# Weights of a mixture of experts in three rings and one halved slot, an attention stage joined with the projections behind it, and a router worked out block by block

## The reference

```python
def second_block(x, ...):
    for l in range(2):
        z = x @ w_in                      # c_q, c_kv, k_rope, sb_qkv, conv_in, fox_qkv, fox_f, gates
        y_a = _mla(...)                   # softmax attention, 4 heads, causal
        y_b = _stick_breaking(...)
        y_c = _conformer_conv(...)        # 31 taps, 256 channels
        y_d = _forgetting_attention(...)
        mix = sum(proj(y) * gate) @ w_o
        x = _layernorm(alpha * x + mix)
        x = _layernorm(alpha * x + _hier_moe(x, ...))

def _hier_moe(h, ...):
    # 4 groups of 8 experts: the best group, in it the best 2 experts
    grp_p, grp_idx = lax.top_k(softmax(xt @ w_rg + b_rg), 1)
    top_p, top_i = lax.top_k(softmax(in_grp), 2)
    weights = grp_p * top_p / sum(top_p)
    # each of 32 experts, on its own tokens: 1024 -> 256 (gate and up) -> 1024 (down), all f32
    hid = silu(xe @ w_gate[e]) * (xe @ w_up[e]);  y = hid @ w_down[e]
```

## Time and profile before

| what | us |
| --- | --- |
| median of 3 runs (2812.06 to 2818.66) | 2812.47 |
| the profiled execution: its own time | 2818.37 |
| its span, first to last instruction | 2816.6 |
| TensorE busy in the span | 2591.9 |
| VectorE, ScalarE, GpSimd busy | 1584.9, 1275.7, 235.3 |

### The profile page before, as it was taken

The page is one execution under the profiler, slowest core; times in us unless marked ns, Lnnn a source line. Parts: engine busy times, 40 slices in busy tenths (PEclk is TensorE's granted clock), DMA queues, the critical chain, the costliest instruction groups (busy, mean ns, idle before and its releaser), DMA issues.

```text
span 2816.6 us, 31757 instructions
## 1 busy us (share of the span) xinstructions
PE 2591.9 (92%) x11554; PEld 1888.7 (67%) x11554; DVE 1584.9 (56%) x2277; ACT 1275.7 (45%) x1881; POOL 235.3 (8%) x201
## 2 busy tenths in 40 slices
PE   6899888899999889999997999988989999799998
PEld 2587665588878567588875666655857887566665
DVE  6646476322223467534456788845854445577775
ACT  5423544422222444533324777725354323377773
POOL 0000000000000010000002333201000000022230
PEclk9899899999999999999998999999999999899999
DMA  9412000222122302022134999851202212299994
GB/s 344 168 60 80 15 1 1 90 90 90 62 73 94 118 33 90 20 101 84 66 122 154 341 331 330 302 187 61 90 30 90 90 60 101 94 329 336 334 332 177
DMA packets 197750, 392.27 MB, mean 139 GB/s; under 512 B 23663, under 2 KB 54399, under 8 KB 197631
## 3 DMA queue, kind: packets, MB, share of 16 engines
q1 hardware_dynamic: 170912, 340.55, 34.5%
q10 hardware_dynamic: 14367, 33.34, 3.1%
q0 software_dynamic: 12352, 16.81, 1.9%
HBM read 386.44 MB, written 29.36 MB: 148 GB/s over the span
## 4 chain that ended last, share of the span: by engine, by line
PE 69%; DMA 10%; DVE 9%; ACT 5%; issue 4%; DVEq 2%; SPq 1%; ACTq 0%; POOL 0%; POOLq 0%; PEld 0%; PEldq 0%
PE banks L198 52%; PE banks L168 8%; DMA ring<-in_w_exp_up 8%; ACT hT_parts L2986 2%; DMA ring<-in_w_mod 1%; PE banks L174 1%; PE banks L1911 1%; PE banks L1919 1%; DVE hT_parts L3089 1%; DVE ring_parts L476 1%; PE banks L1936 1%; SPq L246 1%; PE banks L2220 1%; PE banks L2207 1%; DVE x_res L2539 1%
## 5 line engine op out<-in xcount | busy, mean ns | idle before, releaser
L198 PE MATMUL banks<-hT_parts 128*128 128x512 f32 (+1 forms) x1376 | 545.8, 397 | 0.0
L198 PE MATMUL banks<-arena_parts,hT_parts 128*128 128x512 f32 (+1 forms) x1408 | 527.5, 397 | 12.9 <-DVEq L161 9.1
L198 PE MATMUL banks<-ring_parts,arena_parts 128*80 128x512 f32 (+2 forms) x1296 | 513.7, 396 | 0.0
L198 PE MATMUL banks<-hT_parts,arena_parts 128*128 128x512 f32 (+1 forms) x1248 | 446.8, 398 | 32.2 <-DVE hT_parts L3089 17.4
L198 PE MATMUL banks<-arena_parts,ring_parts 128*128 128x512 f32 (+1 forms) x1168 | 456.4, 391 | 0.0
L198 PE MATMUL banks<-arena_parts 128*128 128x512 f32 (+3 forms) x1280 | 409.9, 392 | 10.5 <-DVEq L161 9.1
L228 DVE TENSOR_TENSOR ring_parts<-ring,hT_parts 128x1024 fp32r<-128x1024 f32 x148 | 183.1, 1237 | 337.3 <-ACT hT_parts L224 333.3
L3092 DVE TENSOR_TENSOR ring_parts<-ring,hT_parts 128x2048 fp32r<-128x2048 f32 x128 | 292.9, 2290 | 119.8 <-ACT hT_parts L2986 119.7
L224 ACT ACTIVATE hT_parts<-ring 128x1024 fp32r<-128x1024 f32 x148 | 156.7, 1058 | 422.0 <-PE banks L198 421.2
L198 PEld LDWEIGHTS banks<-arena_parts,hT_parts 128*128 128x128 f32 x1408 | 267.1, 190 | 77.9 <-DVEq L161 13.8
L2986 ACT ACTIVATE hT_parts<-ring 128x2048 fp32r<-128x2048 f32 x128 | 244.4, 1911 | 159.1 <-DMA ring<-in_w_exp_up 112.9
(11 more groups left out here) (486 smaller groups left out, 3169.5 us busy)
## 6 DMA issues: line engine op xcount, KB each, us to landing
ring<-in_w_exp_gate SPq DMA_DIRECT2D x64, 1024.0 KB, 5.4
ring<-in_w_exp_up SPq DMA_DIRECT2D x64, 1024.0 KB, 8.3
ring<-in_w_exp_down SPq DMA_DIRECT2D x128, 512.0 KB, 4.1
ring<-in_w_in SPq DMA_DIRECT2D x58, 1024.0 KB, 7.3
ring<-in_w_mod SPq DMA_DIRECT2D x24, 1024.0 KB, 12.9
ring<-in_w_gate SPq DMA_DIRECT2D x11, 1024.0 KB, 5.4
ring<-in_w_up SPq DMA_DIRECT2D x11, 1024.0 KB, 8.1
ring<-in_w_down SPq DMA_DIRECT2D x22, 512.0 KB, 4.1
```

The costliest lines, as they stand in the source:

```text
L198: last = nc.tensor.matmul(out, l, r, start=start and i == 0, stop=stop and i == len(products) - 1)
```

## The change

Three parts, all in the two layers.

**Weights of the experts.** Gate and up go through three slots, by b modulo 3. The two halves of the fourth slot hold the downs, by b modulo 2. The loops of all engines hold six experts, in five rounds instead of fifteen. SP asks for gate/up b once that of b-3 is done (it was b-2), and for down b-1 once down b-3 is done.

```diff
         def ex_up(b):
-            return N_EX + max(2 * b - 1, 0)
+            return (3, 0, 2)[b % UPS]
         def ex_down(b):
-            return N_EX + min(2 * b + 2, 2 * NE - 1)
+            return b % 2
...
         def dn_rows(chunks, n):
-            return chunks[n % SLOTS][:, 0:4, :].rearrange("p (f h) n -> p f (h n)", f=2)
+            return chunks[1][:, 4 * n:4 * n + 4, :].rearrange("p (f h) n -> p f (h n)", f=2)
...
-            for n, b in ((N_EX, 0), (N_EX + 1, 1)):
+            for n, b in ((N_EX, 2), (N_EX + 1, 0), (N_EX + 2, 1)):
                 sp.wait_ge(S("chunk_free"), n + 1 + SLOTS * R)
                 up_loads(b, lay * NE + b)
-            sp.wait_ge(S("chunk_free"), N_EX + 3 + SLOTS * R)
-            down_loads(0, lay * NE)
             sp.wait_ge(S("chunk_free"), N_EX + 4 + SLOTS * R)
-            up_loads(2, lay * NE + 2)
-            up_passed(0)
-            down_loads(1, lay * NE + 1)
+            for b in range(2):
+                down_loads(b, lay * NE + b)
...
+            def further(b, first):
+                up_passed(first + (b - UPS))
+                up_loads(b, lay * NE + first + b)
+                down_passed(first + (b - UPS))
+                down_loads(b - 1, lay * NE + first + (b - 1))
...
-            with eng.Fori(0, NE // 2 - 1, 1) as it:
-                for u in range(2):
-                    body(it * 2 + (u + 1), (u + 1) % 2, u + 1, it)
+            with eng.Fori(0, (NE - 2) // UNROLL, 1) as it:
+                for u in range(UNROLL):
+                    body(it * UNROLL + (u + 1), (u + 1) % 2, u + 1, it)
```

```diff
+        def soft_at(tile):
+            return [u for u in range(UNITS + 3) if 4 * u // 3 == tile]
...
+                        tile = 4 * LT * c + LT * q + m
+                        for u in soft_at(tile) if tile < SHARED else ():
+                            mla_step_pe(pe, u)
...
+            for tile in range(SHARED):
+                for u in soft_at(tile):
+                    mla_step_dve(dve, u)
+                if tile % LT == 2:
+                    split(*divmod(tile // LT + 1, 4))
+                if tile in TAP_TILES:
+                    n = TAP_TILES.index(tile)
+                    conv_taps(dve, n, n + 1)
...
-            for c in range(1, 4):
+            for c in (2, 3):
                 unit_run(c, 3, split_and_tap)
+            conv_taps(dve, len(TAP_TILES) + 21, CW)
...
         def pj_pool(pool):
+            pool.wait_ge(S("mla_pv"), H2)
             for m in (s_q, s_v, f_q, f_v):
                 nc.gpsimd.memset(m, 0.0)
```

```diff
             for i in range(1, LT):
-                ln_tile(dve, "ln1", i - 1)
+                ln_tile(dve, "ln1", i - 1, 2)
+                if i == LT - 1:
+                    dve.wait_ge(S("wrt_in"), 4 * 16)
+                    chosen_dve(dve, 0, 1)
                 wo_tile_dve(dve, i)
...
+            ln_tile(dve, "ln1", LT - 1, 2)
+            chosen_dve(dve, 1, LT - 1)
+            dve.wait_ge(S("slots_in"), 1)
+            chosen_dve(dve, LT - 1, LT)
...
+            arrive(pool, "pool")
+            pool.wait_ge(S("placed"), 2)
+            gather_rows(pool, tok_tab[:, 0:1].bitcast(U32), 0).then_inc(S("xg_in0"), 16)
...
                 down_lo(ex_down(b), dn_hi_last).then_inc(S("ex_dl"), 1)
+                over_places_dve(dve)
                 mult(b, 1)
                 h_lo(b, 1)
+                over_slots_dve(dve)
+                gates_dve(dve)
+                over_tables_dve(dve)
+                for j in range(2):
+                    for i in range(LT):
+                        V.tensor_scalar(e_diag[:, j * LT + i, :], ...)
```

More of the change, by code:

```diff
@@ L1867, in mla_dve @@
             k_turned(2)
+            pj_first_dve(dve)
             k_turned(3)
@@ L2373, in wo_tile_pe @@
                            ("chunk_free",) if i + q == 0 else ())
+                if q == 1 and between:
+                    between()
             last.then_inc(S("wo_acc"), 1)
@@ L2528, in ln_stats, with ln_tile @@
                 V.bn_aggr(mv[:, i, :], bn[:, i, :, :]).then_inc(S(which + "_var"), 1)
-        def ln_tile(dve, which, i):
+        def ln_tile(dve, which, i, parts=1):
             V = nc.vector
@@ L2592, in route_pe @@
+                for k in range(KD):
+                    if k % 4 == 0:
+                        pe.wait_ge(S("m_copied"), 2 * i + k // 4 + 1)
+                    last = nc.tensor.matmul(ps[:, 6 + i % 2, 0:40], hT[:, k, tok_of(i)], w_rt[:, k, :], start=(k == 0), stop=(k == KD - 1))
+                last.then_inc(S("lg_acc"), 1)
             for i in range(LT):
-                wo_tile_pe(pe, i)
+                wo_tile_pe(pe, i, (lambda: logits(i - 2)) if i >= 2 else None)
                 if i:
@@ L2612, in route_pe, with count @@
-            for m in range(LT):
-                count(NE * (m + 1), NE * (LT + 1), ones, slice(0, LT - m), start=(m == 0))
-            count(NE, NE * LT, u_lt, slice(1, LT))
-            count(0, NE, u_lt, slice(0, 1), stop=True).then_inc(S("rank_acc"), 1)
-            keep_clock(7, 24)
-            pe.wait_ge(S("placed"), 1)
-            mm(ps[0:CAP, 6, 0:XBLK], [(pl_oh[:, j, :], bl_oh[:, j, :]) for j in range(2 * LT)]).then_inc(S("tab_acc"), 1)
+            def count(c0, c1, which, tiles, start=False, stop=False):
+                return nc.tensor.matmul(ps[:, 5, c0:c1], which, tiles, start=start, stop=stop)
@@ new lines, in route_pe @@
+            pe.wait_ge(S("wo_free"), LT)
+            pe.wait_ge(S("chosen"), 2)
+            for s in range(LT - 1):
+                count(NE * (s + 1), NE * (LT + 1), ones_r, ohs_r[:, s:s + 1, :].to_broadcast([P, LT - s, NE]), start=(s == 0))
+            count(0, NE, before_r, ohs_r[:, 0, :])
+            count(NE, NE * (LT - 1), before_r, ohs_r[:, 1:LT - 1, :])
+            pe.wait_ge(S("m_copied"), 2 * LT)
+            keep_clock(0, 8)
+            pe.wait_ge(S("chosen"), 3)
+            count(NE * LT, NE * (LT + 1), ones_r, ohs_r[:, LT - 1, :])
@@ new lines, in route_pe, with token_of @@
+            count(NE * (LT - 1), NE * LT, before_r, ohs_r[:, LT - 1, :], stop=True).then_inc(S("rank_acc"), 1)
+            keep_clock(0, 6)
+            pe.wait_ge(S("placed"), 1)
+            for j in range(2 * LT):
+                last = nc.tensor.matmul(ps[0:CAP, 4, 0:2 * NE], pl_oh[:, j, :], bl_oh[:, j, :, :].rearrange("p a n -> p (a n)"),
+                                        start=(j == 0), stop=(j == 2 * LT - 1))
+            last.then_inc(S("tab_acc"), 1)
+        def token_of(a, b, n):
+            return tok_f[:, None, a:b].to_broadcast([P, 2, b - a]).rearrange("p j t -> p t j")[:, :, :, None].to_broadcast([P, b - a, 2, n])
@@ L3030, in first @@
                 act.sem_inc(S("ex_yb"), 1)
-                for h in range(2):
-                    w_hi(0, 0, 0, h, True)
                 x_hi(0, 0)
@@ L3127, in first @@
                 x_lo(0, 0)
-                for j in range(2):
-                    for i in range(LT):
-                        V.tensor_scalar(e_diag[:, j * LT + i, :], ident[:, :], e_w[:, j, i:i + 1], None, ALU.mult)
-                dve.drain().then_inc(S("diag_full"), 1)
                 w_lo(1, 1, 0)
@@ L3421, in _ @@
                 for lay in layers("pool"):
-                    for _ in range(2):
-                        rendezvous(pool, "pool")
+                    rendezvous(pool, "pool")
                     pj_pool(pool)
```

649 lines of the change are left out of this document (374 added, 275 removed).

## The result

The changed kernel takes 2764.76 us (median of 4 runs, 2763.02 to 2767.37); the kernel before, in its 4 runs, 2814.96. The ratio is 0.9826, with a 95% interval of 0.9812 to 0.984: 50 us faster. The profiled execution has a span of 2761.3 us, 55.3 less than that of before; the difference to 50 is that the profiled execution of before (2818.37 us) stood 3.4 us over the median of these four runs, while this one, of 2763.02 us, is 1.7 under its own. The prediction's 2757 was 7.8 us low, inside its range.

A forecast was written before the change was run, and what follows sets the result against it. TensorE was two thirds of the chain, with experts waiting for loads and the router for VectorE. Terms -34 - 8 - 26 + 13.6 = -54.8 took 2818.4 to 2763.6 us, so 2757 for the median; range 2732 to 2786.

The forecast's parts named there:

- Experts' loop: Loops over experts in both layers: gain of 16 us in layer 1, 20 in layer 2, taken as 34 together.
- the 9.72 us an expert: Experts' loop: DMA-bound pace, from 3.41 MB an expert at 351 GB/s, against 9.45 us that TensorE needs.
- more gain: Rival: TensorE-bound loops (another 10 us) or a joint stage without its tail (another 7), below 2742 us; chance 0.12.
- Attention with the projections: Joint stage of attention and projections: 125.3 us become 121.1, a gain of 4.2 a layer, 8 in all.
- The stalls of the attention: Joint stage: three stalls of the first and last units, about a microsecond each, 3.0 us added.
- VectorE's taps at the end: Joint stage's end: last six taps take 8.8 us, TensorE's last unit covers 5.5, so 3.4 us added.
- Router: Last layer norm to first expert: VectorE's path ends at 1488.2 against 1501.4, 13 us gained a layer, 26 in all.
- Behind the last expert: Tail after the loop: small instructions moved there cost 6.8 us a layer, 13.6 in all.
- Fourteen instructions, 5.0: Tail: fourteen small VectorE instructions ahead of the last mult, at 0.35 us each, take 5.0 us.
- Stalls at the jumps: Rival, loops of six experts: each of 8 jumps back stalls for a fetch, 3.5 us each, 28 in all, 2782; chance 0.12.
- the slower case of 78: Loops: each jump's fetch queues behind 3.15 MB of weights, eight times 9.7 us, 2835, slower than before; chance 0.05.
- DMA's pace would stay: Rival, experts' loop: DMA's 9% idle is not the slots' doing, only first experts gain, 15 in all, 2777; chance 0.12.

The follow-up runs named there:

- the lead taken back: Changed kernel with gate/up b asked for one expert later, once b-2 is done, as before the change: 2806.14 us, ratio 0.9958 to the kernel before.
- the two added matmuls: Two matmuls without use added to each loop body: 2788.07 us against the changed kernel's 2764.76; in the kernel before, 2819.92 against 2817.29.
- the run with everything: Changed kernel with both tail edits, idle matmuls ahead of the overflow wait, later clearing of three tiles and other convolution tap tiles: 2734.75 us, ratio 0.9716 to before.
- the experiment: Changed kernel with one tile cleared first: 2760.66 us (operation 3.56 us); then also the other three held until VectorE's forget gate is done: 2749.1 us (0.17).
- the run with the choice at once: Changed kernel with experts chosen for all four token tiles in one call behind the last layer norm, instead of three calls: 2780.47 us, ratio 0.9881 to before.
- both waits gone: Changed kernel with overflow places moved behind the last mult and its low part, and the last down weight in expert 29's gate/up slot: 2753.28 us, ratio 0.978 to before.
- the straight loop: Changed kernel with the thirty expert bodies written out straight, without jumps back: 2763.07 us.
- that kernel: Changed kernel with overflow places moved, last down weight in the free gate/up slot, and 24 idle matmuls ahead of the overflow wait, 2 behind: 2753.53 us, ratio 0.9782.
- the overflow places moved: Changed kernel with the fourteen overflow-place instructions moved behind the last mult and its low part: 2756.8 us, ratio 0.9791 to before.

## Why the prediction was right, and where not

The time was right within its range, and so were the signs of all four terms. That the sum came out so close is partly luck: two of its terms were wrong by more than 5 us, in opposite directions. The prediction expected 2763.6 us for an execution like the profiled one, and the profiled one took 2763.02, since the loop's 6 us and the router's 3 of unforeseen gain and the tail's 11 of unforeseen cost nearly cancel. What made 2757 low is the step from there to the median: I took off the 5.9 us by which the profiled execution of before stood over its three runs; with the fourth run it is 3.4, and the changed kernel's profiled execution stands 1.7 under its median and not over it.

**Experts' loop: -34 forecast, -40 measured.** The reason was right and is shown: with the lead taken back the loop takes 318 us. The step that failed is the 9.72 us an expert, "I take 3.41 MB". The loops move 98.8 and 99.3 MB for 31 experts, 3.20 MB each, which at 351 GB/s is 9.1 us, under TensorE's 9.45. So the loop went to TensorE's pace in both layers: layer 2 takes 293.2 us. Layer 1 has the forecast's length, 297.9 us (the forecast's terms add up to 296.8, not 297.5), but not its reason, for TensorE is busy in 293.6 of them. That is the case that I had among "more gain"; the two added matmuls confirm it (+10.7 and +13.2 where a DMA-bound loop would have given 6). The number stood in the prediction: 313.5/31 at 321 GB/s is 3.25 MB. I set it aside for a value nearer to that of one pair of experts, whose 20.5 us carried more than two experts' worth.

**Attention with the projections: -8 forecast, -8.5 measured.** The sum came out, 121.1 against 121.2 us, and TensorE's own share of it is shown: 88.5 + 23.5 is 112.0, and the run with everything has TensorE busy for 112.48. The 9 us around them came out by luck, since they were made of other parts than I wrote. The stalls of the attention (3.0) hardly exist: in the changed kernel the waits inside the stage besides the 4.25 are 0.23 and 0.35 us. Against that the clearing, for which I had 1.1, cost 4.25 of stall and some 2 of clock behind it (with the stall under 1 us the stage is 5.8 us shorter). VectorE's taps at the end cost TensorE a wait of 1.2, for which I had 3.4. What I missed stood in the trace before, though not in the rows that I took: in the same clearing there, a VectorE operation on 128 columns is held for all of it (in layer 2 the same one takes 3.60 us). Timeline of the kernel before, beside the clearing at 1016.74:

```profile
1016.77 7.21 DVE L2099 TENSOR_SCALAR arena_parts<-u_lt 128x128 fp32r<-128x128 f32 x1
```

The Trainium skill, "SBUF — State Buffer", section "Who interferes with whom", says that VectorE and GpSimd share one pair of ports, that whoever has it keeps it for the whole instruction, and that tensor_scalar is among VectorE's operations that can need it. These rows agree in kind, and so do those of the experiment (3.56 and 0.17 us): the instruction that is held is a TENSOR_SCALAR each time. They also show more than the page says: the hold lasted through two memsets in the experiment (3.56 us) and through four in the row above (7.21 us), where one memset takes 1.8.

**Router: -26 forecast, -29 measured.** Right in kind and size, with 2 us a layer between executions of the same code; the run with the choice at once shows that up to 8 us a layer are due to the blocks.

**Behind the last expert: +13.6 forecast, +24.7 measured.** This term was mis-sized by 11 us, the largest error of the prediction. "Fourteen instructions, 5.0" was right (4.6). The first step that failed is what stands ahead of them: I took the last low part of the down weight as standing where it stood, and did not ask where down 31 is loaded to. The diff shows it: `min(2 * b + 2, 2 * NE - 1)` gave it a slot of gate and up, `b % 2` makes it wait for down 29. That is the 3.65 us wait; undone, it is worth 3.1 us in layer 1 and 1.5 in layer 2. The other part is the clock, which the prediction put at nothing: it took the last down and the 34 matmuls at their old lengths. TensorE, 7.46 and 6.08 us idle, came back at a granted clock of 0.50 and 0.65: the last down took 5.4 and 4.3 us instead of 2.97, the 34 matmuls 9.4 and 10.4 instead of 8.0. And with both waits gone the tail is still 8.7 and 8.5 us longer than before, where 6.8 was forecast with the fourteen instructions in the way: the row of small instructions, with what it costs in clock, is dearer than I took it.

**The rivals.** Stalls at the jumps, both as a rival of 28 us and as the slower case of 78, are refuted by the straight loop: nothing gained, and 11 fetches where the loop of six has 2 or 3. (The first was also added up wrongly: 2757 and 28 are 2785, not 2782. And by the chances as given the stated range leaves out 0.12, not 0.2.) The page of the Trainium skill that I weighed ("Runtime: NRT & Kernel Launch", "Instruction fetch mechanics") speaks of a stall where the target lies outside the window; no run here shows one with 276 matmuls to a body. That DMA's pace would stay is refuted by its share of 0.94 and 0.96 and by loops of 298 and 293 us. "More gain" happened in the loop and was eaten by the tail.

**Open.** The same loop in the same code takes from 292.6 to 299.5 us in different executions and layers; what makes it so was not found. Nor was it tried to let the results be asked for before the overflow is known, which by the row at 1807.17 is what ends the tail of that kernel; the kernel with everything has the same wait for the results (3.62 and 3.78 us), and its sum takes 12.9 and 13.4 us instead of 10.46.

## What to carry to other kernels

A ring with one more slot is worth what the idle share of DMA says, up to the next bound; work out both paces, from bytes counted over a long stretch and not over one period, and take the slower. When slots are dealt out anew, follow the first and the last item apart, since their slots had exceptions. When work is moved behind a loop, put the clock-keeping matmuls where TensorE now idles, and not where they were.

## What was not expected of the hardware

A VectorE operation on 16 columns (TENSOR_SCALAR) beside a memset of GpSimd took 1.81, 3.49 and 3.56 us, and 0.17 without; it ends when one of the memsets ends, not always the first. Convolution taps (SCALAR_TENSOR_TENSOR) beside the same memsets took no longer than elsewhere. A loop body of 276 matmuls was run five times with 2 or 3 instruction fetches in all; written out straight, it had 11. And idle time on TensorE at the end of the loop is paid twice: behind 7.46 us of it the twelve matmuls of the last down took 5.37 us instead of 2.97, and the 34 after those, behind a second wait of 3.23 us, 9.39 instead of 8.00. The price does not grow with the length of the wait: behind 4.20 us they took 5.38, behind 6.08 us 4.34, and behind 0.96 us (with the overflow places moved, layer 2) 4.54; without a wait of that kind 2.95.
